# Opening norm of a hybrid decoder layer: lead weights in two halves, meta rows scaled by ScalarE, narrow unread products

## The reference, cut to what matters

```python
def rms_norm(x, g, eps=NORM_EPS):
    xf = x.astype(jnp.float32)
    y = xf * lax.rsqrt(jnp.mean(xf * xf, axis=-1, keepdims=True) + eps)
    return (y * g.astype(jnp.float32)).astype(x.dtype)
...
h = jnp.concatenate([meta, x], axis=1)
h = h + hybrid_mixer(rms_norm(h, norm1_g[l]), w_in[l], ...)
h = h + hierarchical_moe(rms_norm(h, norm2_g[l]), ...)
...
u = n @ w_in
u_shift = token_shift(u[..., :SHIFT_W], rwkv_mu)
```

## Time and profile before

| what | value |
|---|---|
| median of 3 runs | 813.61 us (813.19 to 816.47) |
| profiled execution, its own time | 812.5 us |
| its span, first to last instruction | 810.7 us |
| mean granted TensorE clock | 0.996 |
| TensorE busy | 789.3 us, 97% of the span |
| VectorE, ScalarE, GpSimd busy | 36%, 25%, 12% |

### The profile page before, as it was taken

The page is one execution under the profiler, slowest core; times in us unless marked ns, Lnnn a source line. Parts: engine busy times, 40 slices in busy tenths (PEclk is TensorE's granted clock), DMA queues, the critical chain, the costliest instruction groups (busy, mean ns, idle before and its releaser), DMA issues.

```text
span 810.7 us, 16955 instructions
## 1 busy us (share of the span) xinstructions
PE 789.3 (97%) x7312; PEld 464.6 (57%) x7312; DVE 289.6 (36%) x547; ACT 205.9 (25%) x408; POOL 101.0 (12%) x213
## 2 busy tenths in 40 slices
PE   9999999999999899899999999999999999999994
PEld 8888888877777554455555555544444563333331
DVE  5333940033333334554544243245311443122112
ACT  4224301122253312433342122540033301011000
POOL 8850000000020100222100000000000011221211
PEclk9999999999999999999999999999999999999998
DMA  7511316200000010528112130455561389999972
GB/s 206 126 52 53 104 53 185 76 3 3 3 5 3 3 29 27 129 54 223 52 53 53 53 78 1 173 155 165 229 263 52 113 298 401 403 384 386 387 272 85
DMA packets 76154, 109.29 MB, mean 135 GB/s; under 512 B 17035, under 2 KB 61211, under 8 KB 71984
## 3 DMA queue, kind: packets, MB, share of 16 engines
q1 hardware_dynamic: 71456, 93.22, 33.7%
q0 software_dynamic: 4624, 14.99, 6.3%
HBM read 99.79 MB, written 10.50 MB: 136 GB/s over the span
## 4 chain that ended last, share of the span: by engine, by line
PE 92%; DMA 4%; DVE 2%; issue 1%; ACT 0%; POOL 0%; SPq 0%; POOLq 0%; DVEq 0%; ACTq 0%
PE ps L1561 21%; PE ps L1455 9%; PE ps L1538 9%; PE ps L1916 9%; PE ps L1849 7%; PE ps L1629 7%; PE ps L1798 6%; PE ps L1543 5%; PE ps L1942 4%; DMA arena<-in_moe_w_up 4%; PE ps L1734 2%; PE ps L1781 2%; PE ps L1439 1%; PE ps L1765 1%; PE ps L1805 1%; PE ps L1885 1%
## 5 line engine op out<-in xcount | busy, mean ns | idle before, releaser
L1561 PE MATMUL ps<-arena 128*128 128x512 f32 x304 | 141.1, 605 | 0.0
L1561 PEld LDWEIGHTS ps<-arena 128*128 128x128 f32 x304 | 54.3, 189 | 58.9 <-issue 58.0
L1916 PE MATMUL ps<-arena 128*32 128x512 f32 x624 | 84.7, 591 | 1.7 <-DMA arena<-in_moe_w_up 1.2
L1455 PE MATMUL ps<-arena 128*128 128x264 f32 x320 | 72.7, 386 | 0.0
L1455 PEld LDWEIGHTS ps<-arena 128*128 128x128 f32 x320 | 60.0, 189 | 11.5 <-ACT arena L762 0.7
L1629 PEld LDWEIGHTS ps<-arena 64*64 64x64 f32 x2784 | 51.6, 134 | 20.3 <-issue 15.0
L1538 PE MATMUL ps<-arena,h 128*128 128x264 f32 x256 | 61.3, 391 | 0.0
L1629 PE MATMUL ps<-arena 64*64 64x64 f32 x2784 | 56.9, 220 | 4.1 <-DVE arena L1119 2.1
L1849 PE MATMUL ps<-arena 128*128 128x512 f32 x128 | 56.0, 594 | 0.0
L1916 PEld LDWEIGHTS ps<-arena 128*32 128x32 f32 x624 | 24.3, 108 | 49.2 <-issue 49.2
L1538 PEld LDWEIGHTS ps<-arena,h 128*128 128x128 f32 x256 | 47.3, 189 | 8.5
(11 more groups left out here) (339 smaller groups left out, 975.7 us busy)
## 6 DMA issues: line engine op xcount, KB each, us to landing
arena<-in_moe_w_down SPq DMA_DIRECT2D x32, 512.0 KB, 15.3
arena<-in_moe_w_gate SPq DMA_DIRECT2D x13, 1024.0 KB, 12.2
arena<-in_moe_w_up SPq DMA_DIRECT2D x13, 1024.0 KB, 16.0
arena<-in_w_in SPq DMA_DIRECT2D x19, 512.0 KB, 3.9
arena<-in_w_in SPq DMA_DIRECT2D x5, 1024.0 KB, 5.9
h<-in_x SPq DMA_DIRECT2D x8, 512.0 KB, 5.9
arena<-in_w_out SPq DMA_DIRECT2D x1, 4096.0 KB, 13.1
h<-in_w_in SPq DMA_DIRECT2D x3, 1024.0 KB, 5.4
```

Source lines behind the costliest of these rows:

```text
L1455: ins = mm(ps[:, 2 * (n % 2) + hf, 0:HALF], w[:, c, j * P:(j + 1) * P], nT[:, c, hf * HALF:(hf + 1) * HALF], start=(c == 0), stop=(c == DC ...
L1561: ins = mm(ps[:, gate_bank(n), :], weights_of_gate(n)[:, c, :], nT[:, c, META:L], start=(c == 0), stop=(c == DC - 1))
L1916: ins = mm(ps[rs, bank, :].rearrange("p (h n) -> p h n", h=2), xgT[:, s, c, rs], w1[ws][:, :, c, :], start=(c == 0), stop=(c == DC - 1))
```

## The change

`WARM` becomes four numbers, (8, 16, 5, 9): 8 unread products of 128 columns, then 16, 5 and 9 that move 32 columns against the same 128x128 identity. SP issues tile 1 ahead of the gain, then the first half of the lead piece, tiles 2 and 3, the second half of the lead piece, piece 1, `muc`, the other parameters, piece 2. The meta rows' squares and sum become one VectorE instruction. Their scaling moves to ScalarE, behind tile 1's root. TensorE turns tile 0, then tile 1, then the meta rows. VectorE copies tile 1 in two halves around the meta copy. Chunk 0's and chunk 1's products for the first half of `nT` are cut in two parts each, with tiles 2 and 3 turned among them. The wait for all parameters moves to where they are used. `mu` has a semaphore of its own.

```diff
--- before.py
+++ after.py
@@ -40,7 +40,7 @@
 C_G = C_F + FH
 PIECE = 256
 RING = 3
-WARM = (27, 3, 9)
+WARM = (8, 16, 5, 9)
 RING_W = FW + FH
 CH = 64
 NCH = SEQ // CH
@@ -57,7 +57,7 @@
 EARLY_GATES = 5
 EARLY_SLOTS = 3
 SHIFT_ORDER = (4, 1, 2, 0, 3)
-PARAMS_A, PARAMS_B = 16 * 8, 16 * 16
+PARAMS_A, PARAMS_B = 16 * 7, 16 * 16
 META_FILL = (("gram", 3), ("H1", 1), ("G1", 2), ("H2", 1), ("G2", 2), ("H3", 1), ("G3", 2), ("U", 2), ("S", 0))
 TURN_FILL = 5
 LEVEL_FILL = 3
@@ -373,26 +373,35 @@
         def _(sp):
             sp.dma_start(h[:, 0, :], x[0:P, :]).then_inc(sem("tile_in0"), 16)
             sp.dma_start(metax[0:META, :], meta).then_inc(sem("meta_in"), 16)
+
+            def load_tile(t):
+                sp.dma_start(h[:, t, :], x[t * P:(t + 1) * P, :]).then_inc(sem(f"tile_in{t}"), 16)
+
+            def load_lead(j, s):
+                cols = slice(j * P, (j + 1) * P)
+                sp.dma_start(slot(0)[:, :, cols], wv[:, :, pieces[0][1][0][0] + j * P:pieces[0][1][0][0] + (j + 1) * P]).then_inc(s, 16)
+            load_tile(1)
             sp.dma_start(g1c, g1.rearrange("(c p) -> p c", p=P)).then_inc(sem("g1_in"), 16)
-            for t in range(1, NT):
-                sp.dma_start(h[:, t, :], x[t * P:(t + 1) * P, :]).then_inc(sem(f"tile_in{t}"), 16)
+            load_lead(0, sem("lead_in"))
+            load_tile(2)
+            load_tile(3)
+            load_lead(1, slot_sem(0))
 
             def load_piece(i):
                 col = 0
                 for c0, n in pieces[i][1]:
                     sp.dma_start(slot(i)[:, :, col:col + n], wv[:, :, c0:c0 + n]).then_inc(slot_sem(i), 16)
                     col += n
-            load_piece(0)
+            load_piece(1)
+            sp.dma_start(muc, mu.rearrange("(c p) -> p c", p=P)).then_inc(sem("mu_in"), 16)
             par = sem("params_in")
-            for dst, src in ((muc, mu.rearrange("(c p) -> p c", p=P)),
-                             (w0c, w0.rearrange("(c p) -> p c", p=P)), (a0c, a0.rearrange("(c p) -> p c", p=P)),
+            for dst, src in ((w0c, w0.rearrange("(c p) -> p c", p=P)), (a0c, a0.rearrange("(c p) -> p c", p=P)),
                              (up_w[0:64, :], w_up), (up_w[64:128, :], a_up),
                              (kkc, k_k.rearrange("(c h) d -> (h d) c", h=2)),
                              (kac, k_a.rearrange("(c h) d -> (h d) c", h=2)),
                              (rkc, r_k.rearrange("(c h) d -> (h d) c", h=2))):
                 sp.dma_start(dst, src).then_inc(par, 16)
-            for i in range(1, RING):
-                load_piece(i)
+            load_piece(2)
             par = sem("g1_in")
             sp.wait_ge(par, 16)
             sp.wait_ge(sem("rw_clear"), 1)
@@ -413,7 +422,7 @@
                 elif i < N_HOME:
                     sp.wait_ge(sem("fill_psum"), 1 + last_group(i - 3))
                 if i == N_SHIFT:
-                    sp.wait_ge(sem("xs_ready"), NT + 1)
+                    sp.wait_ge(sem("xs_ready"), NT)
                 if i == N_HOME:
                     sp.wait_ge(sem("bonus_moved"), 1)
                 load_piece(i)
@@ -701,9 +710,10 @@
             for t in range(NT):
                 act.wait_ge(sem(f"tile_in{t}"), 16)
                 first_norm(stat[:, t:t + 1], xs[:, t, :], h[:, t, :], P)
-                if t == 0:
+                if t == 1:
                     act.wait_ge(sem("ss_ready"), 1)
                     root(stat[0:META, 4:5], META)
+                    done(a.activation(metax[0:META, :], metax[0:META, :], ACT.Copy, scale=stat[0:META, 4:5]), "meta_scaled")
             act.wait_ge(sem("g1_in"), 16)
             act.wait_ge(sem("xT_psum"), NT + 1)
             t = NT - 1
@@ -711,7 +721,6 @@
                 o = 1024 * t + c * P
                 ins = a.activation(nT[:, c, META + t * P:META + (t + 1) * P], psf[:, o:o + P], ACT.Copy, scale=g1c[:, c:c + 1])
             done(ins, "nT_high")
-            act.wait_ge(sem("params_in"), PARAMS_A)
 
             out_n = [0]
 
@@ -746,6 +755,8 @@
 
 
             def decay_gate(c):
+                if c == 0:
+                    act.wait_ge(sem("params_in"), PARAMS_A)
                 act.wait_ge(sem("wa_psum"), 2 * c + 1)
                 pin = ps[:, 4:6, 0:HALF]
                 done(a.activation(ta[:, c, :].rearrange("p (a b) -> p a b", a=2), pin, ACT.Sigmoid, bias=w0c[:, c:c + 1]), "wa_used")
@@ -981,37 +992,37 @@
             done(v.memset(rw_pad[:], 0.0), "rw_clear")
             for j in range(SC):
                 done(v.memset(U[:, j, 0:1], 0.0))
-            gain = lambda c1, n: g1c[:, 0:c1].rearrange("p (c a) -> p c a", a=1).broadcast_to([P, c1, n])
-
-            def chunks_out(t, c1):
-                dve.wait_ge(sem("xT_psum"), t + 1 if t == 0 else t + 2)
-                done(tt(nT[:, 0:c1, META + t * P:META + (t + 1) * P],
-                        psf[:, 1024 * t:1024 * t + c1 * P].rearrange("p (c n) -> p c n", c=c1), gain(c1, P), ALU.mult), "nT_low")
+            gain = lambda c0, c1, n: g1c[:, c0:c1].rearrange("p (c a) -> p c a", a=1).broadcast_to([P, c1 - c0, n])
+
+            def chunks_out(t, c0, c1):
+                dve.wait_ge(sem("xT_psum"), t + 1 if t < 2 else t + 2)
+                done(tt(nT[:, c0:c1, META + t * P:META + (t + 1) * P], psf[:, 1024 * t + c0 * P:1024 * t + c1 * P].rearrange("p (c n) -> p c n", c=c1 - c0),
+                        gain(c0, c1, P), ALU.mult), "nT_low")
+
+            def scaled(t):
+                dve.wait_ge(sem("rstd_ready"), t + 1 if t < 2 else t + 2)
+                done(ts(xs[:, t, :], h[:, t, :], stat[:, t:t + 1], None, ALU.mult), "xs_ready")
             squares = tmp_shift[0:META, :, :].rearrange("p a b -> p (a b)")[:, 0:D]
             dve.wait_ge(sem("meta_in"), 16)
-            done(tt(squares, metax[0:META, :], metax[0:META, :], ALU.mult))
-            done(v.tensor_reduce(stat[0:META, 4:5], squares, mybir.AxisListType.X, ALU.add), "ss_ready")
-            for t in range(NT):
-                if t == 2:
-                    chunks_out(1, DC)
-                dve.wait_ge(sem("rstd_ready"), t + 1 if t == 0 else t + 2)
-                done(ts(xs[:, t, :], h[:, t, :], stat[:, t:t + 1], None, ALU.mult), "xs_ready")
-                if t == 0:
-                    dve.wait_ge(sem("rstd_ready"), 2)
-                    done(ts(metax[0:META, :], metax[0:META, :], stat[0:META, 4:5], None, ALU.mult), "xs_ready")
-                    dve.wait_ge(sem("g1_in"), 16)
-                if t in (1, 3):
-                    chunks_out(t - 1, DC)
-                if t == 1:
-                    dve.wait_ge(sem("xT_psum"), 2)
-                    done(tt(nT[:, :, 0:META], ps[:, 7, 0:DC * META].rearrange("p (c n) -> p c n", c=DC), gain(DC, META), ALU.mult), "nT_meta")
-            chunks_out(NT - 1, T_SPLIT)
+            done(v.tensor_tensor_reduce(squares, metax[0:META, :], metax[0:META, :], 1.0, 0.0, ALU.mult, ALU.add, stat[0:META, 4:5]), "ss_ready")
+            scaled(0)
+            scaled(1)
+            dve.wait_ge(sem("g1_in"), 16)
+            chunks_out(0, 0, DC)
+            chunks_out(1, 0, DC // 2)
+            dve.wait_ge(sem("xT_psum"), 3)
+            done(tt(nT[:, :, 0:META], ps[:, 7, 0:DC * META].rearrange("p (c n) -> p c n", c=DC), gain(0, DC, META), ALU.mult), "nT_meta")
+            chunks_out(1, DC // 2, DC)
+            scaled(2)
+            scaled(3)
+            chunks_out(2, 0, DC)
+            chunks_out(3, 0, T_SPLIT)
             r_, k_, v_ = U[:, 0:3, 1:], U[:, 3:6, 1:], U[:, 6:9, 1:]
             AL, BL, KL = (z[:, :, 0:L] for z in (At, Bt, Kt))
             halves_of = lambda z: z.rearrange("p (a b) -> p a b", a=2)
             done(v.memset(Pc[:], 1.0))
 
-            dve.wait_ge(sem("params_in"), PARAMS_A)
+            dve.wait_ge(sem("mu_in"), 16)
 
             def mixed(n, *s_):
                 j = chunk_at[n]
@@ -1034,6 +1045,7 @@
 
             for n in range(3):
                 mixed(n, *(["wd_mixed"] if n == 1 else []))
+            dve.wait_ge(sem("params_in"), PARAMS_A)
             dve.wait_ge(sem("consts_ready"), 1)
             for c in range(RC):
                 mixed(3 + c)
@@ -1434,13 +1446,14 @@
             mm = nc.tensor.matmul
             tr = nc.tensor.transpose
             pe.wait_ge(sem("ident_ready"), 1)
-            def unread_first(count):
+            def unread_first(count, n=2 * META):
                 for _ in range(count):
-                    mm(ps[:, 5, 0:P], ident[:], ident[:], start=True, stop=True)
-            unread_first(WARM[0])
+                    mm(ps[:, 5, 0:n], ident[:], ident[:, 0:n], start=True, stop=True)
+            unread_first(WARM[0], P)
+            unread_first(WARM[1])
 
             def turned(t):
-                pe.wait_ge(sem("xs_ready"), 1 if t == 0 else t + 2)
+                pe.wait_ge(sem("xs_ready"), t + 1)
                 if t == NT - 1:
                     pe.wait_ge(sem("nT_meta"), 1)
                 for c in range(DC):
@@ -1448,37 +1461,47 @@
```

(30 more changed lines are left out.)

## The result

| | kernel before | changed kernel |
|---|---|---|
| median, us (lowest to highest, 6 runs each) | 813.95 (812.74 to 816.47) | 822.74 (819.27 to 825.09) |
| profiled execution, us | 812.5 | 819.27 |
| its span, us | 810.7 | 817.5 |

The ratio is 1.0109, with a 95% interval of 1.0089 to 1.0129. The change makes the kernel 1.1% slower, 8.8 us. The prediction (813.3 us, range 811.3 to 816.5) was wrong, and the time is almost that of its rival (a), 823.3 us, which had a chance of 0.10. The profiled execution of the changed kernel is the fastest of its six, so its rows show less than the median's loss.

The account below looks back on a forecast made before the run. It took TensorE's instruction order and pace to bound the opening, with data ready slightly earlier. Fewer, narrow unread products and hidden norm and transfers gave -0.3 us: 813.61 to 813.3 us, range 811.3 to 816.5.

Parts of the forecast that it names:

- rival (a): Opening: narrow products don't raise the clock, which stays low until the real products; 10.0 us less 0.3, 823.3 us; chance 0.10.
- The price of a narrow instruction: Unread products in the opening: 0.113 us per 32-column instruction at the high clock, as for 128 columns, 0.213 at the low.
- rival (c): Opening: weight load blind to the clock, narrow ones 0.113 us throughout, real products 0.5 us earlier still; 812.8 us; chance 0.12.
- The data side: Opening: moved norm, split real products and reordered transfers all ready before TensorE wants them, first real product covered by 1.5 us.
- the sum of -0.3 us: Whole forecast: all gain in the opening, first real product at 14.5 to 14.7 us instead of 14.92, carried to the end.
- with the clock rising at 5.9 again: Opening: TensorE's clock goes from 1.2 to 2.4 GHz at 5.9 us as before, pricing later narrow instructions at 0.113 us.
- (b): Opening: the clock rises a few us late, at 8 to 13 us; costs 1 to 3.3 us, 814.3 to 816.6; chance 0.18.
- a stretch with TensorE busy for 2.87 of 5.0 us keeps 1.00: Profile row of the kernel before, cited against the clock staying low, with the caveat that it shows keeping, not rising.

Follow-up runs that it names:

- before_narrow: Kernel before, order and counts kept, but 19 of its first 27 unread products and the later 3 and 9 move 32 columns: 823.34 us, ratio 1.0107.
- control: The kernel before, unchanged, run again for a second profile and a spread: 812.69 us, ratio 0.9992.
- later_narrow: Changed kernel with the first 8 and 16 unread products wide, only the 5 and 9 behind tile 0 narrow: 815.79 us, ratio 1.0026.
- few_wide: Changed kernel with fewer unread products, `WARM = (8, 11, 4, 3)`, all 128 columns wide: 817.83 us, ratio 1.0058.
- before_hold: Kernel before with unread products put into two later TensorE waits, near 329 and 645 us: 812.53 us, ratio 0.9994.
- all_wide_hold: Changed kernel with all unread products 128 columns wide and two later TensorE waits filled with unread products: 813.22 us, ratio 0.999.

## Why the prediction was wrong, point by point

**The price of a narrow instruction: right.** 0.113 us was used for the high clock and 0.213 for the low; starts are 0.111 us apart from 5.1 to 8.4 us and 0.214 behind 15.14. The weight load's record goes from 192 to 333 ns with the clock, so rival (c), one price at both clocks, is out. The Trainium skill (TensorE: Matmul & The Clock Gate, LDWEIGHTS) gives for a load of 128 columns, by its formula, 107 ns with no mention of the clock. The traces agree with it at neither clock.

**The data side: right.** Norm, pieces and transfers are hidden; TensorE waits for none of them. Tile 0 was turned at 8.56 instead of the predicted 9.0, since the clock rose sooner. With wide products the first real one is at 14.45, so the sum of -0.3 us was a fair one for an opening in which the clock stays high.

**The clock: the step that failed.** It is "with the clock rising at 5.9 again". The text treated the rise as an event with a time, after which the clock stays. The runs show that it can be taken back: risen at 5.1, fallen at 8.5 with TensorE busy without a gap, back at 22.1. The 10 + 18 narrow instructions and 16 transposes of 128x128 behind the fall cost about double, the eight small ones 0.96 us against 0.60, and the first real products double too: 5.7 us in this profile, where the sum had -0.3. Neither rival (a) nor (b) had this form; both knew only a rise that comes late. That is the form of `before_narrow`'s profile and, by the mean clocks, probably of half the changed kernel's executions. The cause that they named, narrow products in place of wide ones, was the right one. The price worked out for (a) was within 0.05 us of `before_narrow`, but it was made for another order of the opening, so that close a match is in part luck.

**The weighing of (a): the reason for 0.10.** The argument against it was that a stretch with TensorE busy for 2.87 of 5.0 us keeps 1.00. Two things were wrong. Busy time did not tell the two cases apart: ahead of the fall PE is busy for 3.30 of 3.30 us by its records, more than in the earlier trace rows. And the earlier trace rows is one execution; `control` shows that the clock falls behind that same stretch in others. The row bore no weight. The Trainium skill (TensorE: Matmul & The Clock Gate, Part 4) says that transposes don't engage the full clock. That was not what decided: in `later_narrow` 5.6 us of transposes and narrow products kept the high pace, eight transposes in 1.04 us. Whether transposes alone would raise it no run here shows.

**The neutral rest of the change: not covered.** The prediction asked of each step what it does to the order and the data. It did not ask what a few instructions fewer do to the code behind them. That is about 0.18% here, 1.5 us, several times the 0.3 us that the change was to gain.

**What stays open.** Why some instruction packets land late: the stalls are tied to late packets, but no run shows what delays one packet and not the next, and the stalls are only 0.8 of the 1.4 us by which the 64x64 stretch differs between the two places. Why 32 narrow instructions in a row lost the clock and 28 among transposes did not; each is shown by one profile, and the rise lies at another distance from them. What made five of `few_wide`'s six executions slow. Whether filling the waits is worth anything to the kernel before: 0.9994 [0.9977, 1.001] allows both nothing and the 0.12% of the estimate.

## What to carry to other kernels

Making filler narrow saves no time where the weight load sets the pace (0.11 us per instruction for 32 columns as for 128 here), and it can cost the clock that the filler is there to hold, for 14 us and more in this kernel. A clock that one profile shows as kept may be lost in many other executions (about half of them here): read the pace of the instructions, in more than one profile, before a row is used as evidence that nothing happens. The profiled execution can also be the fastest of a spread, as it was for the changed kernel and for `few_wide`: compare its time with the median before its rows explain the median. When an edit of the opening changes the number of instructions, compare with a version that has the same number, or 0.2% of placement is taken for an effect of the edit.

## What the runs showed of the hardware

- The clock fell with PE and PEld busy for 3.30 of 3.30 us on 128x32 products, and stayed high on 128x64 in most executions. The same narrow products mixed with transposes kept it.
- The first rise came between 4.6 (`before_hold`) and 7.2 us (`all_wide_hold`) in the fourteen profiles whose filler ahead of tile 0 was all wide, by the traces' clock records. Where the clock was low at the first real product, it rose 3.1 (changed kernel) and 4.6 us (`before_narrow`) after it.
- Around a wait of 2.1 us in the middle of the kernel some executions had 3.4 us at 0.50, between two stretches at 1.00: seven of twelve profiles, and none of six with the wait filled. It cost about 1.7 us.
- The granted clock reads 1.00 before the first change that is recorded, at 0.21 us per instruction as at 0.11.
- Three instructions more or fewer ahead of a dense stretch of small products changed the time by about 0.18%. The issue stalls there, up to 1.1 us each, all stood at the same place in TensorE's blocks of 256 instructions, 1.2 to 1.6 us behind the end of a 16 KB instruction packet.
